# Both merge-gate projections as a two-by-two block product with seven block multiplications, and token staging through four buffers

## The reference

```python
u = rms_norm(h, g_pre)                                   # (B, L, 1024)
proj = jnp.einsum('bld,dn->bln', u, w_in)
(c_b, c_c, c_x, c_z, q, k, v, r, lr_f, lr_b, m_a, m_b) = jnp.split(proj, ...)
...                                                      # a short convolution mixer, a bidirectional gated linear attention
p_conv = jnp.einsum('blc,cd->bld', y_conv, w_out_c)
p_gla = jnp.einsum('blc,cd->bld', y_gla, w_out_g)
merged = jax.nn.sigmoid(m_a) * p_conv + jax.nn.sigmoid(m_b) * p_gla
out = jnp.einsum('bld,de->ble', merged, w_out)
return h + rms_norm(out, g_post)
```

## Time and profile before

| What | Value |
|---|---|
| Time, median of 3 runs | 2955.36 us (2952.26 to 2955.38) |
| Span of the profiled execution, slowest core | 2951.6 us (fastest core 2941.7 us) |
| PE busy | 2897.5 us, 98% |
| DVE busy | 1572.8 us, 53% |
| ACT busy | 1301.6 us, 44% |
| POOL busy | 836.6 us, 28% |
| Moved by DMA | 347.19 MB, mean 118 GB/s |

### The profile page before, as it was taken

The page is one execution under the profiler, slowest core; times in us unless marked ns, Lnnn a source line. Parts: engine busy times, 40 slices in busy tenths (PEclk is TensorE's granted clock), DMA queues, the critical chain, the costliest instruction groups (busy, mean ns, idle before and its releaser), DMA issues.

```text
span 2951.6 us, 53626 instructions; the slowest of 8 cores (2941.7 to 2951.6 us)
## 1 busy us (share of the span) xinstructions
PE 2897.5 (98%) x16316; PEld 1491.5 (51%) x16316; DVE 1572.8 (53%) x2415; ACT 1301.6 (44%) x2492; POOL 836.6 (28%) x1286
## 2 busy tenths in 40 slices
PE   6999999999999999999999999999999999999998
PEld 3565644444465554444456655444446555544443
DVE  4766652451677773163277776226338777523523
ACT  5766651321466662132266665223136666412212
POOL 3343333221432221141243222123124222211212
PEclk9999999999999999999999999999999999999999
DMA  7686557842632233283363334246245323323323
GB/s 181 133 138 115 127 120 161 234 131 77 179 107 72 75 96 99 76 239 101 95 184 85 78 85 112 68 143 197 76 122 152 84 72 93 101 76 107 119 76 125
DMA packets 322327, 347.19 MB, mean 118 GB/s; under 512 B 206064, under 2 KB 209136, under 8 KB 321536
## 3 DMA queue, kind: packets, MB, share of 16 engines
q1 hardware_dynamic: 308512, 318.39, 38.8%
q0 software_dynamic: 13536, 25.37, 6.1%
HBM read 265.67 MB, written 59.31 MB: 110 GB/s over the span
## 4 chain that ended last, share of the span: by engine, by line
PE 97%; DMA 1%; DVE 1%; issue 1%; POOL 0%; ACT 0%; SPq 0%; DVEq 0%; POOLq 0%; ACTq 0%
PE ps L478 96%; DMA sb_onT<-x 0%; DMA sb_KT<-sb_GR 0%; PE ps L483 0%; DMA sb_ycT<-x 0%; POOL sb_stat L513 0%; POOL sb_stat L657 0%; SPq L535 0%; DVE sb_onT L508 0%; DVE sb_TB L508 0%; POOL sb_SB L513 0%; ACT ps L495 0%; DVE sb_ycX L508 0%; ACT L495 0%; DVE sb_ycT L504 0%
## 5 line engine op out<-in xcount | busy, mean ns | idle before, releaser
L478 PE MATMUL ps<-sb_uT,sb_W 128*128 128x512 bf16 (+2 forms) x8960 | 1869.8, 367 | 0.7 <-ACT sb_CS L495 0.4
L478 PEld LDWEIGHTS ps<-sb_uT,sb_W 128*128 128x128 bf16 (+1 forms) x8960 | 820.5, 98 | 938.6 <-issue 16.7
L495 ACT ACTIVATE sb_CS<-ps 128x512 f32<-128x512 f32 (+2 forms) x640 | 349.7, 552 | 919.5 <-PE ps L478 917.7
L508 DVE SCALAR_TENSOR_TENSOR sb_CS<-sb_CS,ps 128x512 f32<-128x512 f32 x256 | 176.1, 688 | 658.4 <-PE ps L478 655.3
L504 POOL TENSOR_TENSOR sb_GR<-sb_CS 128x512 bf16<-128x512 f32 x128 | 162.2, 1267 | 742.7 <-DVE sb_CS L508 742.2
L478 PE MATMUL ps<-sb_GR 128*128 128x512 bf16 (+2 forms) x1792 | 349.0, 318 | 0.0
L478 PE MATMUL ps<-sb_V,sb_uT 128*128 128x256 bf16 x2048 | 238.1, 274 | 0.0
L508 DVE SCALAR_TENSOR_TENSOR sb_CS<-sb_CS,sb_convw 128x512 f32<-128x512 bf16 x256 | 218.9, 865 | 35.2 <-ACT sb_CS L495 23.0
L478 PEld LDWEIGHTS ps<-sb_GR 128*128 128x128 bf16 x1792 | 164.2, 98 | 136.6 <-issue 0.7
L478 PE MATMUL ps<-sb_onT,sb_W 128*128 128x512 bf16 x1024 | 232.2, 379 | 0.7 <-DVE sb_onT L508 0.7
L504 POOL TENSOR_TENSOR sb_CS<-sb_CS 128x512 f32<-128x512 f32 x128 | 161.8, 1265 | 201.0 <-DVE sb_CS L508 170.0
(11 more groups left out here) (114 smaller groups left out, 2525.1 us busy)
## 6 DMA issues: line engine op xcount, KB each, us to landing
sb_W<-wsc SPq DMA_DIRECT2D x496, 256.0 KB, 2.6
sb_onT<-x SPq DMA_DIRECT2D x50, 512.0 KB, 5.6
sb_W<-w_all POOLq DMA_DIRECT2D x80, 256.0 KB, 6.1
sb_GR<-x SPq DMA_DIRECT2D x40, 512.0 KB, 5.3
wsc<-sb_W SPq DMA_DIRECT2D x80, 256.0 KB, 5.7
y<-sb_GR SPq DMA_DIRECT2D x32, 512.0 KB, 3.3
sb_ycT<-x SPq DMA_DIRECT2D x32, 512.0 KB, 5.2
y<-sb_ycT SPq DMA_DIRECT2D x32, 512.0 KB, 3.4
```

Source lines behind the costliest of these rows:

```text
L478: S.add("pe", lambda e: e.matmul(out, lhsT=lhsT, rhs=rhs, start=start, stop=stop), r, w, cost=max(0.025, free_n(rhs) / 2400.0 + 0.0025) / ...
L495: S.add("act", lambda e: e.activation(out=out, in_=in_, func=func, **kw), r, w, table=TABLE.get(func), cost=0.17 + 0.82e-3 * free_n(in_) + ...
L508: S.add("dve", lambda e: e.scalar_tensor_tensor(out=out, in0=in0, scalar=scalar, in1=in1, op0=op0, op1=op1), r, w, cost=0.21 + 1.05e-3 * f ...
```

## The change

With the tokens of a half split in two blocks of 512 and the 1024 input features split in two blocks of 512, the two gates of one output block d are a product of a 2 x 2 arrangement of weight blocks with a 2 x 2 arrangement of token blocks. The change computes it with seven block products in Winograd's form, in place of eight. Each product is 4 matmuls of 128x128 weights with 128x512 tokens.

- `tsums` makes four differences of token blocks (`TT`, bf16), once for each half, on DVE. They lie in the regions `AT` and `V`, so the two `AT` buffers for staging tokens go (four instead of six), `usA` moves to `TF` and `KT`, and the first load of v of a batch waits for the last gate unit of the batch before.
- The weights' sums are made by `sums_w` during the first half of batch 0, which keeps the plain form, and are stored in `wst`, from which the other seven half-batches load them ("S" blocks; "Y" is half of the mb weights).
- `Seven` does one output block. p1's bank is copied out by ACT (`sd1`); p5 and p6 have p1's result added on DVE into `sd5` and `sd2`. p2 then accumulates onto p1's bank, p3 onto p5's, p7 onto p6's, and p4 on top of p7. `fin` takes the tanh, after adding `sd2`, `sd5` or `sd1` on DVE for three of the four results. The order of a block is p1 p5 p6 p2 p3 p7, oc first half, p4, oc second half, og.
- The gate weights move to the pool `W2` (four loads a block), oc and og move to `W1`. The merge is done in place in `ta` and `tb2`.

The diff, cut to its core:

```diff
@@ -356,6 +356,7 @@
+    wst_d = nc.dram_tensor("wst", [8 * 128 * 8, 256], BF16, kind="Internal").ap()
...
-        def mm(out, lhsT, rhs, start, stop, r, w, share=1):
-            S.add("pe", lambda e: e.matmul(out, lhsT=lhsT, rhs=rhs, start=start, stop=stop), r, w,
+        def mm(out, lhsT, rhs, start, stop, r, w, share=1, more=False):
+            S.add("pe", lambda e: e.matmul(out, lhsT=lhsT, rhs=rhs, start=start, stop=stop, skip_group_check=more), r, w,
...
@@ -553,6 +554,13 @@
+        def wcols(blk):
+            return 1024 if blk[0] == "S" else 512 if blk[0] == "Y" else BLK_OFF[blk][1]
+        def ssrc(pair, z):
+            return wst_d[pair * 1024:(pair + 1) * 1024, :].rearrange("(p a) n -> p (a n)", p=128)[:, z * 1024:(z + 1) * 1024]
...
@@ -560,16 +568,17 @@ class WPool
+            def reserve(self, blk, after=()):
                 n = len(self.seq)
-                first = blk not in first_use
+                first = blk[0] not in "SY" and blk not in first_use
                 first_use.add(blk)
                 self.seq.append((blk, first))
-                put("W" + self.name, lambda: self.load(n), None, [("SA", 0, {"W1": 1, "V": 2, "W2": 3}[self.name])] if n == 0 else ())
+                put("W" + self.name, lambda: self.load(n), None,
+                    [("SA", 0, {"W1": 1, "V": 2, "W2": 3}[self.name])] if n == 0 else after)
                 return (self, n)
...
+                if blk[0] == "S":
+                    _, pair, z = blk
+                    dma("sp", ap, ssrc(pair, z), [("wst", pair, z)], k, ("w", self.name, s), 1 << 18)
+                elif blk[0] == "Y":
+                    dma("sp", ap, wsrc(wsc_d, blk[1])[:, 512:1024], [("wsc", blk[1])], k, ("w", self.name, s), 1 << 17)
+                elif first:
...
@@ -618,7 +632,10 @@
-        p2 = {n: [Buf("CS", (i * 2 + z) * 2048, 2048) for z in range(2)] for i, n in enumerate(("ta", "t1", "tb", "t2"))}
+        ta = [Buf("CS", z * 2048, 2048) for z in range(2)]
+        tb2 = [Buf("CS", 4096 + z * 2048, 2048) for z in range(2)]
+        sd1, sd2, sd5 = (Buf("CS", 8192 + z * 2048, 2048) for z in range(3))
+        TT = [Buf("AT", 0, 4096), Buf("AT", 4096, 4096), Buf("AT", 8192, 4096), Buf("V", 0, 4096)]
...
-        usA = [kraw, qraw]
+        usA = [Buf("TF", 0, 2048), Buf("KT", 0, 2048)]
...
-                            vh = wv.reserve(("v", s))
+                            vh = wv.reserve(("v", s), [("mb", b - 1, 1, 7, 1)] if b and not s else ())
...
@@ -1304,16 +1321,132 @@
             return late
+        def uTv(k0, t):
+            ap = REG["uT"][:, :].rearrange("p (k t) -> p k t", k=8)[:, k0:k0 + 4, t:t + 512]
+            return ap, [g for k in range(k0, k0 + 4) for g in uT[k](BF16, t, 512)[1]]
+        def tsums(b, hh, gates_):
+            t0 = hh * 1024
+            b11, b12, b21, b22 = uTv(0, t0), uTv(0, t0 + 512), uTv(4, t0), uTv(4, t0 + 512)
+            o = []
+            for bf in TT:
+                ap, k = bf(BF16)
+                o.append((ap.rearrange("p (k t) -> p k t", k=4), k))
+            for i, (dst, x, y) in enumerate([(o[0], b12, b11), (o[1], b22, o[0]), (o[2], b22, b12), (o[3], b21, o[1])]):
+                put("TT", lambda dst=dst, x=x, y=y: tt("dve", dst[0], x[0], y[0], ALU.subtract, x[1] + y[1], dst[1]),
+                    ("TT", b, hh, i), gates_[i])
+        def sums_w(hx, hy, pair):
+            x1, xk1 = wbuf(hx)(BF16, 0, 512)
+            x2, xk2 = wbuf(hx)(BF16, 512, 512)
+            y1, yk1 = wbuf(hy)(BF16, 0, 512)
+            y2, yk2 = wbuf(hy)(BF16, 512, 512)
+            S1, S2 = sd1(BF16, 0, 512), sd1(BF16, 512, 512)
+            S4, S3 = sd2(BF16, 0, 512), sd2(BF16, 512, 512)
+            tt("dve", S1[0], y1, y2, ALU.add, yk1 + yk2, S1[1])
+            tt("dve", S2[0], S1[0], x1, ALU.subtract, S1[1] + xk1, S2[1])
+            tt("dve", S4[0], x2, S2[0], ALU.subtract, xk2 + S2[1], S4[1])
+            tt("dve", S3[0], x1, y1, ALU.subtract, xk1 + yk1, S3[1])
+            for z, bf in enumerate((sd1, sd2)):
+                ap, k = bf(BF16)
+                dma("sp", ssrc(pair, z), ap, k, [("wst", pair, z)], ("ws", z), 1 << 18)
+        class Seven:
+            def __init__(self, me, pair, X, Y, t0, fin):
+                self.me, self.t0, self.fin = me, t0, fin
+                self.h = [w2.reserve(X), w2.reserve(("S", pair, 0)), w2.reserve(("S", pair, 1)), w2.reserve(("Y", Y))]
+            def mul(self, bk, hi, wo, rhs, first):
+                bank, bkk = bk
+                wb = wbuf(self.h[hi])
+                for k in range(4):
+                    w_ap, wkk = wb(BF16, wo + k * 128, 128)
+                    r_ap, rk = rhs(k)
+                    mm(bank[:, 0:512], w_ap, r_ap, first and k == 0, k == 3, wkk + rk, bkk, more=not first)
+            def u(self, k0, t):
+                return lambda k: uT[k0 + k](BF16, self.t0 + t, 512)
+            def tt(self, i):
+                return lambda k: TT[i](BF16, k * 512, 512)
+            def plus(self, out, bk, s_):
+                s_ap, s_k = s_(F32)
+                tt("dve", out[0], bk[0][:, 0:512], s_ap, ALU.add, bk[1] + s_k, out[1])
+            def p1(self):
+                a = G["s", "a"] = nps(True)
+                self.mul(a, 0, 0, self.u(0, 0), True)
+                o_ap, o_k = sd1(F32)
+                act(o_ap, a[0][:, 0:512], AF.Copy, a[1], o_k)
+            def p5(self):
+                G["s", "e"] = nps(True)
+                self.mul(G["s", "e"], 1, 0, self.tt(0), True)
+                self.plus(sd5(F32), G["s", "e"], sd1)
+            def p6(self):
+                G["s", "b"] = nps(True)
+                self.mul(G["s", "b"], 1, 512, self.tt(1), True)
+                self.plus(sd2(F32), G["s", "b"], sd1)
+                rel(self.h[1])
+            def p2(self):
+                a = G["s", "a"]
+                self.mul(a, 0, 512, self.u(4, 0), False)
+                rel(self.h[0])
+                self.fin(0, 0, a)
+                drop(a[1])
+            def p3(self):
+                e = G["s", "e"]
+                self.mul(e, 2, 0, self.u(4, 512), False)
+                self.fin(0, 1, e, sd2)
+                drop(e[1])
+            def p7(self):
+                b_ = G["s", "b"]
+                self.mul(b_, 2, 512, self.tt(2), False)
+                rel(self.h[2])
+                self.fin(1, 1, b_, sd5)
+            def p4(self):
+                b_ = G["s", "b"]
+                self.mul(b_, 3, 0, self.tt(3), False)
+                rel(self.h[3])
+                self.fin(1, 0, b_, sd1)
+                drop(b_[1])
         def stage6(b, hh, late=()):
             t0 = hh * 1024
-
-            def gate(h, d, s, n):
+            plain = b == 0 and hh == 0
+            def tanh(dst, in_, r):
+                a_ap, a_k = dst(F32)
+                act(a_ap, in_, AF.Tanh, r, a_k, scale=0.5)
+            def gate(h, d, s, n, hx=None):
                 bank, bk = nps()
                 proj(h, 0, 128, t0 + s * 512, 512, bank, bk)
-                a_ap, a_k = p2[n][s](F32)
-                act(a_ap, bank[:, 0:512], AF.Tanh, bk, a_k, scale=0.5)
-                if s == 1:
+                tanh((ta if n == "ma" else tb2)[s], bank[:, 0:512], bk)
+                if s == 1 and n == "mb":
+                    sums_w(hx, h, d)
+                    rel(hx)
                     rel(h)
+            def fin(f, s, bk, s_=None):
+                dst = (ta, tb2)[f][s]
+                if s_ is None:
+                    tanh(dst, bk[0][:, 0:512], bk[1])
+                    return
+                d_ap, d_k = dst(F32)
+                s_ap, s_k = s_(F32)
+                tt("dve", d_ap, bk[0][:, 0:512], s_ap, ALU.add, bk[1] + s_k, d_k)
+                tanh(dst, d_ap, d_k)
             def outp(h, d, s, n, src):
                 bank, bk = nps()
@@ -1322,36 +1455,51 @@
                     w_ap, wkk = wb(BF16, c * 128, 128)
                     y_ap, yk = src(c, s)
                     mm(bank[:, 0:512], w_ap, y_ap, c == 0, c == 7, wkk + yk, bk)
-                a_ap, a_k = p2["ta" if n == "t1" else "tb"][s](F32)
-                o_ap, o_k = p2[n][s](F32)
-                stt(o_ap, a_ap, 1.0, bank[:, 0:512], ALU.add, ALU.mult, bk + a_k, o_k)
-                if n == "t2":
-                    t_ap, t_k = p2["t1"][s](F32)
+                a_ap, a_k = (ta if n == "oc" else tb2)[s](F32)
+                stt(a_ap, a_ap, 1.0, bank[:, 0:512], ALU.add, ALU.mult, bk + a_k, a_k)
+                if n == "og":
+                    t_ap, t_k = ta[s](F32)
                     m_ap, m_k = mT[d](BF16, s * 512, 512)
-                    tt("pool", m_ap, t_ap, o_ap, ALU.add, t_k + o_k, m_k)
+                    tt("pool", m_ap, t_ap, a_ap, ALU.add, t_k + a_k, m_k)
                 if s == 1:
                     rel(h)
             ysrc = lambda c, s: ycT(hh, c)(BF16, s * 512, 512)
             osrc = lambda c, s: onv(c, hh * 8 + 4 * s, 4)
-            hs = {}
-            seq = [(n, d) for d in range(8) for n in ("ma", "oc", "mb", "og")]
```

(61 more changed lines are left out.)

6 lines of the change are left out of this document (2 added, 4 removed).

## The result

The changed kernel takes 2921.3 us in the median of three runs (2920.65 to 2921.41), before 2955.37 us: a ratio of 0.9884, 95% interval 0.9866 to 0.9902, so 1.2% faster. Forecast was 2912 us, range 2903 to 2927: right in direction, with the time inside the range, and 9 us too good. The time lies outside the 2906 to 2917 us that the forecast alone was given; the range holds it because it also takes in the rival of dearer seams.

A forecast was written before the change was run, and what follows sets the result against it. The prediction took PE's number of matmuls to bound the kernel. Span 2951.6 - 48.3 + 3.2 + 2 = 2908.5 us; with the median 3.8 us above the span, 2912 us, range 2903 to 2927 us.

The forecast's parts named there:

- the forecast alone: Whole kernel: the summed forecast of 2912 us, given 2906 to 2917 us at chance 0.70.
- rival of dearer seams: First stage's late weights at 7.5 us, three batch boundaries at up to 3.45 each: 2928 us, chance 0.12.
- The matmuls: Seven gate half-batches: 28 matmuls instead of 32 per block, 224 fewer at unchanged pitch, 48.3 us saved.
- Waits inside a block: Changed blocks: by the chain of hand-overs, every wait is covered by 0.48 us or more of other matmuls; cost nothing.
- the break-even: Changed blocks: at a DVE pass of 1.36 us, PE waits 0.86 us and the block is back at 13.81 us.
- The differences: Second half's four token differences, 1.47 us each, delay DVE's sums in the last first-half block: 1.07 us, 3.2 in three batches.
- batch 0, whose four come together behind the last gate unit: Batch 0's token differences, released together, lie on no bank that PE waits for: no cost taken.
- The first gate stage: Batch 0's first half: the first mb block's write-back and load may come late, 0 to 7.5 us once; 2 us taken.
- The head loops: First-half differences run beside them on DVE: nothing, and up to 1.47 us each if the recurrence waits.
- Staging and the batch boundaries: Four token buffers instead of six, last eight tiles released 3.45 us later: up to 10.4 us possible, 0 taken.
- Around the span: Whole kernel: the median of the runs stands 3.8 us above the profiled span, turning 2908.5 into 2912 us.
- The slower one by DVE: Changed blocks: sums come back late and p3, p7 and p4 pile up; at 1.47 us a pass, 2977 us; chance 0.04.
- the one by the clock: Gate stages: new waits make PE's clock fall; one block in seven at 1.2 GHz gives 3016 us; chance 0.03.

The follow-up runs named there:

- experiment 5: The changed kernel with p4 right behind p7 in every block, the first oc unit after it: 2991.06 us in one run.
- experiment 6: The changed kernel with each of a block's five new DVE passes made twice in a row: 3006.8 us in one run.
- experiment 7: The changed kernel without the last three DVE sums of each block, tanh taken straight from the bank: 2918.0 and 2919.3 us, ratio 0.9874.
- experiment 3: The kernel before with only the weight pools swapped, gates in W2 and outputs in W1: 2963.65 to 2966.26 us, ratio 1.0034.
- experiment 2: The changed kernel with the first gate stage's ma and mb weights in a third pool in AT, its oc and og in W2: 2911.4 to 2912.0 us.
- experiment 1: The kernel before with only the staging part: four token buffers, usA in TF and KT: 2954.2 to 2956.1 us, ratio 1.0002.
- experiment 9: The changed kernel with each first half's token differences moved behind the recurrence's last outputs: 2928.7 and 2929.8 us, ratio 0.991.
- experiment 4: Its first kernel: the kernel before with only the late first load of v: 2962.9 to 2966.6 us, ratio 1.0032.
- second kernel of experiment 4: The kernel of experiment 2 with V freed and v loaded behind its own batch's first eight staged tiles: 2911.0 to 2912.5 us, ratio 0.9855.

## Why the prediction came out 9 us too good

**The matmuls**: right to the last place. 224 went, and a block takes 12.95 us.

**Waits inside a block**: right. No wait in a plain block, and experiments 5 to 7 show each side: the cover gone costs what the chain says, the pass doubled passes the break-even, the sums gone change nothing in a block. One exception was not foreseen: p4 of block d=0, where the recurrence's last work is still in DVE's queue. PE's timeline in batch 1, then DVE's:

```profile
1146.88 0.38 PE L479 MATMUL ps<-sb_V,sb_W 128*128 128x512 bf16 x1 [0.60 <-DVE sb_CS L505]
```

```profile
1145.27 0.88 DVE L514 TENSOR_SCALAR sb_ON<-ps,sb_stat 128x256 bf16<-128x256 f32 x2 [0.40 <-POOL sb_stat L674]
1146.06 0.68 DVE L505 TENSOR_TENSOR sb_CS<-ps,sb_CS 128x512 f32<-128x512 f32 x1
```

The sum that p4 needs starts at 1146.06, behind the recurrence's `ON`, which itself waited 0.40 us for POOL; p4 follows 0.14 us after the sum, the hand-over taken in the prediction.

**The differences**: the term was 3.2 us, for 1.07 a batch. Each takes 1.22 us, not 1.47 (twice 0.74 was the upper bound), and block d=7 loses 0.4 us: all that the other 14 blocks of a batch lose in the three batches is 2.0 us, some of it elsewhere.

```profile
1240.95 1.22 DVE L505 TENSOR_TENSOR sb_AT<-sb_uT 128x2048 bf16<-128x2048 bf16 x1
...
1242.92 1.02 PE L479 MATMUL ps<-sb_AT,sb_W 128*128 128x512 bf16 x4 [0.23 <-DVE sb_CS L505]
```

For batch 0, whose four come together behind the last gate unit, the prediction took nothing, on the ground that they lie on no bank that PE waits for. That is a failed step too, of 1.3 us: they fill DVE from 539.44 us on, og's last products stand behind them, and POOL's sums and a tile of the output projection behind these (DVE, POOL and PE):

```profile
543.04 1.22 DVE L505 TENSOR_TENSOR sb_V<-sb_uT,sb_AT 128x2048 bf16<-128x2048 bf16 x1
544.17 1.28 DVE L509 SCALAR_TENSOR_TENSOR sb_CS<-sb_CS,ps 128x512 f32<-128x512 f32 x2
545.00 2.48 POOL L505 TENSOR_TENSOR sb_GR<-sb_CS 128x512 bf16<-128x512 f32 x2 [12.60 <-DVE sb_CS L509]
546.41 2.10 PE L479 MATMUL ps<-sb_GR 128*128 128x512 bf16 x9 [1.06 <-POOL sb_GR L505]
```

og starts at 540.22, so by the hand-over of 0.41 us its first product was due at 542.36 and came at 544.17.

**The first gate stage** is the step that failed first: 2 us were taken, bounds 0 to 7.5, for the first mb block; the slowest core lost 7.7 in the stage. PE's timeline in it, then POOL's:

```profile
425.10 10.52 PE L479 MATMUL ps<-sb_uT,sb_W 128*128 128x512 bf16 x48
...
437.59 0.38 PE L479 MATMUL ps<-sb_onT,sb_W 128*128 128x512 bf16 x1 [0.68 <-DVE sb_onT L509]
438.91 2.10 PE L479 MATMUL ps<-sb_onT,sb_W 128*128 128x512 bf16 x9 [0.94 <-DVE sb_onT L509]
...
449.15 3.61 PE L479 MATMUL ps<-sb_uT,sb_W 128*128 128x512 bf16 x16 [1.23 <-DMA sb_W<-w_all]
...
456.06 3.62 PE L479 MATMUL ps<-sb_uT,sb_W 128*128 128x512 bf16 x16
462.64 5.23 PE L479 MATMUL ps<-sb_ycT,sb_W 128*128 128x512 bf16 x16 [2.96 <-DMA sb_W<-w_all]
467.70 3.62 PE L479 MATMUL ps<-sb_uT,sb_W 128*128 128x512 bf16 x16
```

```profile
455.51 1.26 POOL L505 TENSOR_TENSOR sb_GR<-sb_CS 128x512 bf16<-128x512 f32 x1 [8.09 <-DVE sb_CS L509]
456.73 0.57 POOL L536 DMA_DIRECT2D sb_W<-w_all  x1
```

The block that the prediction priced, mb of d=0, did not wait: it begins the first row, and by the semaphores in the trace its load was issued at 394.43 us and landed at 399.40. Three others did. og of d=0 waits for the recurrence's last products on DVE and loses 1.9 us where it lost 0.3 before; the change also drops the line that put ma of d=1 ahead of it, so it starts 64 matmuls behind oc of d=0 instead of 80. mb of d=1 loses 1.4 us: it gets the buffer of ma of d=0, whose write-back was issued at 429.10 behind the stores of the weights' sums and landed at 441.65, and its own load, issued at 442.25, landed at 448.91.

The largest wait is that of the oc block of d=2, which the prediction did not look at: oc and og had gone from a ring of five buffers to one of three. Its casting load is the next instruction on POOL after the merge sum of og d=1, and is issued as that sum ends, at 456.73 us; POOL had sat before the sum for 8.09 us, for DVE's product of that og. The buffer, that of og d=0, had been free for 11.3 us: the write-back that the load waits for landed at 445.41, and PE was done with og of d=0 at 441. So the place in POOL's queue made the load late. The load took 5.66 us; issued at 445.41 it would have landed near 451 us (an estimate from these numbers), and oc's place was 459.51. It landed at 462.39, and oc starts 3.13 us late. Then the 16 matmuls take 5.06 us from start to start where 3.45 is the pitch, since the clock had fallen while PE stood (columns of the earlier trace rows):

```profile
462.60:466.00 3.40, 3.36 (x9) 1.19 (x10) 0.00 (x0) 0.00 (x0) 0.00 (x0) 0.51 1.09 182
466.00:470.00 4.00, 4.00 (x20) 1.82 (x19) 2.44 (x5) 0.26 (x1) 0.00 (x0) 1.00 0.49 123
```

0.51 is the 1.2 GHz level. 3.13 + 1.61 = 4.7 of the stage's 7.7 us are this one load; mb of d=1 has 1.4, og of d=0 1.6. Experiment 3 has the same wait, at the same place and with the same rows on POOL, from the swap alone (there the write-back landed at 443.19 and the load was issued at 456.49); experiment 2 takes it away. The clock fell on two of the eight cores, and they are the two that lost most (cores 3 and 6, 7.7 and 9.2 us; the others 2.2 to 4.0). Why the planner put the load behind that sum is not shown.

**The head loops** are the second failed step: the prediction gave them nothing, and they lost 6.9 us. In batch 1 PE's waits in that stretch are these (before: `SB` 0.7 in 1, ACT's `CS` 0.4, `onT` 0.2):

```profile
PE ps L479 <- POOL sb_SB L514: 2.1, 3, 0.7
PE ps L479 <- DVE sb_CS L505: 0.6, 1, 0.6
PE ps L479 <- DVE sb_onT L509: 0.5, 1, 0.5
```

3.2 against 1.3 us: 1.9 of the 2.3, and each stop is some 0.16 us longer than its row says, because a matmul's modelled end (379 ns after its start) lies behind the pitch of 216. Experiment 7 takes 1.1 of the 2.3 away (0.8 and 0.5 in the next two batches), by the p4 of block d=0 among others; the waits for `SB`, a state that POOL scales for the recurrence, stay. Staging, the differences and the late v do not make them (experiments 1, 9, 4); the swap of pools alone does (experiment 3), to the same size. In experiment 3 PE's order leaves that of the kernel before right behind batch 0's last og, and the changed kernel differs at that place too. Before, then the changed kernel:

```profile
758.92 4.09 PE L478 MATMUL ps<-sb_uT,sb_W 128*16 128x512 bf16 x40
762.84 3.62 PE L478 MATMUL ps<-sb_GR 128*128 128x512 bf16 x16
```

```profile
759.12 10.52 PE L479 MATMUL ps<-sb_GR 128*128 128x512 bf16 x48
769.58 5.46 PE L479 MATMUL ps<-sb_uT,sb_W 128*16 128x512 bf16 x48
```

The next batch's first unit starts 3.6 us behind the start of the last og before, 10.6 in experiment 3 and 13.9 in the changed kernel; the output projection (`GR`) goes first. But the second kernel of experiment 4 starts it at 7.0, and its head loops are as long as those of experiment 2, so the later start does not set the loss by itself. Why the new order puts units of the head loops where `SB` is late stays open: a version with the later gates in `W1` and their loads counted anew was not tried.

**Staging and the batch boundaries**: right at nothing. PE has no wait from 1440 to 1640 us in either kernel, and experiment 1 is even.

**Around the span**: 3.8 us were added, taken from before; the profiled execution of after lies 1.6 above its span. That takes 2 us off the miss: 11.1 in the span, 9.3 in the time.

**The rivals**: seams that cost more, at 2928, is nearest to what happened. Its first half, weights late in the first stage by 7.5 us, came true in size (7.7 on the slowest core), by luck: at other blocks, and the largest wait by a place in a queue and not by the transfers; its second, 10.4 us at the batch boundaries, did not, and the head loops took 6.9 in its place. The slower one by DVE is real as a mechanism, and experiments 5 and 6 show what keeps it away; the one by the clock was not seen in the gate stages, even with a stop in each block.

## What to carry to other kernels

A product with fewer multiplications pays in full on a matmul-bound stage, as long as every bank that another engine reads between two products has other matmuls behind it; write that chain out in hand-overs, for here it held to 0.14 us, and look at the first and last block, where neighbours share DVE's queue. When blocks change pools, follow every load of the first pass, and its place in the queue of the engine that issues it, not only the transfer's own time: here one load stood behind a sum for 11 us after its buffer was free, and cost more than all the waits inside the blocks. In a kernel that a planner orders, undo each part by itself on the chip, since a part that looks free can move the order by 10 us, and compare all cores, since those of one execution lie as far apart.

## What the runs showed of the hardware that was not expected

A difference of two 128x2048 bf16 tiles takes 1.22 us on DVE. A sum of two 128x512 bf16 tiles takes 0.42 us, and the operation on two of 128x1024 that the prediction doubled 0.68 in the median (its means are 0.74 before and 0.70 after, since some take longer). So each 512 elements cost 0.27 us, and some 0.15 us do not depend on the length. PE's stops near 1 us in every block left the granted clock at 1.00. Longer single stops in the first stage did not all act alike: behind one of 2.96 us the clock stood at 0.51 for 3.4 us, behind one of 2.35 on core 6 at 0.56, and behind one of 2.84 on core 0 and one of 3.21 on core 6 at 1.00.
